# A decoder trunk with a mixture of experts on one core: the gathered rows of experts 2 to 8 turned by VectorE, the router in two products a chunk, constant transposes on TensorE

## The reference, cut to what matters

```python
def moe(xn, w_router, wg, wu, wd):
    t = xn.reshape(-1, D)
    logits = (t @ w_router).astype(jnp.float32)
    top_vals, top_idx = lax.top_k(logits, TOP_K)          # TOP_K = 2 of N_EXPERTS = 8
    gates = jax.nn.softmax(top_vals, axis=-1)
    comb = jnp.einsum('nk,nke->ne', gates, jax.nn.one_hot(top_idx, N_EXPERTS, dtype=jnp.float32))
    for e in range(N_EXPERTS):                            # wg, wu 2048 x 1408, wd 1408 x 2048
        y = y + comb[:, e:e + 1] * swiglu(t, wg[e], wu[e], wd[e])
```

## Time and profile before

| | |
|---|---|
| median of 3 runs | 1921.18 us (1921.08 to 1922.72) |
| the profiled execution: its time | 1918.63 us |
| the profiled execution: its span | 1916.6 us |
| TensorE matmuls, weight loads | busy 1906.1 us (99%), 1587.2 us (83%) |
| VectorE, ScalarE, GpSimd | 1348.1 us (70%), 1160.1 us (61%), 136.6 us (7%) |
| mean granted TensorE clock | 0.999 |
| HBM read, written | 495.33 MB, 13.64 MB: 266 GB/s over the span |

### The profile page before, as it was taken

One profiled execution on the slowest core, in us unless ns is written; L12 is line 12 of the kernel. 1 busy time (PEld: TensorE's weight loads), 2 busy tenths in 40 slices (PEclk: granted clock), 3 DMA queues, 4 the chain that ended last, 5 costly groups with the idle time before them and its releaser, 6 DMA issues.

```text
span 1916.6 us, 25622 instructions
## 1 busy us (share of the span) xinstructions
PE 1906.1 (99%) x8984; PEld 1587.2 (83%) x8984; DVE 1348.1 (70%) x1574; ACT 1160.1 (61%) x1490; POOL 136.6 (7%) x152
## 2 busy tenths in 40 slices
PE   9999999999999999999999999999999999999998
PEld 7888888888888888888888888888888888888887
DVE  8876654545455445444659688898988998988996
ACT  7656543434343344333645567787887878787885
POOL 8300000000000000000200000010100100000101
PEclk9999999999999999999999999999999999999999
DMA  9644555565565555555555468999999999999997
GB/s 357 197 159 161 178 189 191 189 197 187 188 192 192 190 190 190 194 190 188 180 189 167 147 209 319 384 393 388 392 389 393 385 399 380 402 378 401 380 394 259
DMA packets 141571, 510.13 MB, mean 266 GB/s; under 512 B 15937, under 2 KB 15953, under 8 KB 140081
## 3 DMA queue, kind: packets, MB, share of 16 engines
q1 hardware_dynamic: 134288, 486.64, 70.4%
q0 software_dynamic: 7200, 22.39, 4.6%
HBM read 495.33 MB, written 13.64 MB: 266 GB/s over the span
## 4 chain that ended last, share of the span: by engine, by line
PE 98%; DMA 1%; DVE 0%; issue 0%; ACT 0%; SPq 0%; POOLq 0%; DVEq 0%
PE main L617 31%; PE main L619 31%; PE main L618 31%; PE transpose L951 1%; PE transpose L635 1%; PE transpose L816 1%; PE transpose L991 0%; PE transpose L934 0%; DMA raw_pieces<-in_ffn_moe 0%; DMA raw_pieces<-in_w_in 0%; PE transpose L657 0%; DVE w_low L1396 0%; PE transpose L712 0%; PE transpose L713 0%; PE transpose L711 0%
## 5 line engine op out<-in xcount | busy, mean ns | idle before, releaser
L1396 DVE TENSOR_TENSOR w_low<-raw_pieces,w_high 128x1024 fp32r<-128x1024 f32 x919 | 1095.1, 1224 | 420.3 <-ACT w_high L1052 413.8
L1052 ACT ACTIVATE w_high<-raw_pieces 128x1024 fp32r<-128x1024 f32 x919 | 948.2, 1058 | 249.9 <-DMA raw_pieces<-in_ffn_dense 126.2
L617 PE MATMUL main<-w_high,xT_high 128*128 128x512 f32 (+1 forms) x1856 | 719.2, 388 | 0.7 <-DVE w_low L1517 0.3
L619 PE MATMUL main<-w_high,xT_low 128*128 128x512 f32 (+1 forms) x1856 | 710.0, 383 | 0.0
L618 PE MATMUL main<-w_low,xT_high 128*128 128x512 f32 (+1 forms) x1856 | 709.1, 382 | 0.0
L619 PEld LDWEIGHTS main<-w_high,xT_low 128*128 128x128 f32 x1856 | 348.8, 188 | 68.6
L617 PEld LDWEIGHTS main<-w_high,xT_high 128*128 128x128 f32 x1856 | 349.1, 188 | 66.2 <-issue 1.6
L618 PEld LDWEIGHTS main<-w_low,xT_high 128*128 128x128 f32 x1856 | 349.3, 188 | 65.0
L617 PE MATMUL main<-w_high,hT_high 128*128 128x512 f32 x832 | 329.9, 397 | 0.6 <-DVE hT_low L1792 0.6
L619 PE MATMUL main<-w_high,hT_low 128*128 128x512 f32 x832 | 324.6, 390 | 0.0
L618 PE MATMUL main<-w_low,hT_high 128*128 128x512 f32 x832 | 324.1, 390 | 0.0
(11 more groups left out here) (231 smaller groups left out, 816.0 us busy)
## 6 DMA issues: line engine op xcount, KB each, us to landing
raw_pieces<-in_ffn_moe SPq DMA_DIRECT2D x528, 512.0 KB, 6.0
raw_pieces<-in_ffn_dense SPq DMA_DIRECT2D x264, 512.0 KB, 3.5
raw_pieces<-in_w_in SPq DMA_DIRECT2D x96, 512.0 KB, 3.5
raw_pieces<-in_w_out SPq DMA_DIRECT2D x32, 512.0 KB, 3.5
x_resid<-in_x SPq DMA_DIRECT2D x4, 512.0 KB, 14.5
out_x<-x_resid POOLq DMA_DIRECT2D x4, 512.0 KB, 4.5
xn_rows<-token_major POOLq DMA_DIRECT2D x2, 1024.0 KB, 5.5
token_major<-in_x_t SPq DMA_DIRECT2D x1, 1024.0 KB, 9.5
```

Of the source, the lines that this page charges most:

```text
L617: pe.matmul(out_ap, lh[ls], rh[rs], start=first, stop=False)
L619: return pe.matmul(out_ap, ll[ls], rh[rs], start=False, stop=last)
L1052: act.activation(WH[:, piece % RING, :], RAWS[:, piece % RING, :], ACT.Copy).then_inc(high_done, 1)
L1396: dve.tensor_tensor(WL[:, piece % RING, :], RAWS[:, piece % RING, :], WH[:, piece % RING, :], ALU.subtract).then_inc(low_done, 1)
```

## The change

- **Gather.** `xn_rows` has four rows of 2 KB for each token. `XN` is stored with the element inside a chunk first and the chunk second (`p t m k`), so VectorE writes it (L1605 before), ScalarE scales it and TensorE reads it with a step of 16 elements. POOL issues four indirect transfers of 128 quarter-rows instead of one of 128 rows; each takes one quarter of every slot's row, for slots in runs of 32. VectorE turns each quarter in one instruction of 32 x 32 blocks, SBUF to SBUF, into `XTR`, which lies where the low part lies; ScalarE copies two halves of 128 x 1024 as the high part, and VectorE makes the low part in two halves. The 16 transposes on TensorE, and their PSUM banks, are gone from the loop.
- **Row numbers.** `slot_values` makes one more small product pair (4 columns), and VectorE makes a second selection (`SELR`) and one more copy for it at step 8, and a few small tables before the loop.
- **Router.** High and low weights stand side by side in one operand of 16 columns: two products a chunk, the logits' two parts added by two small products each tile. The last block of the output projection runs tile by tile, and its last four chunks are turned per tile through the `main` banks. The last two multiplications with the gain stand later, `keep_busy` writes a `transpose` bank and has two more calls (4 and 7 transposes). ScalarE scales `XN` block by block, and TensorE's first gather waits for each block alone.

```diff
+RUN = 32
+RUNS = P // RUN
+BUSY_LAST, BUSY_COPY, BUSY_RANKS, BUSY_SLOTS = 4, 7, 18, 8
+E_QUARTER = {42: 0, 44: 1, 46: 2, 48: 3}
+E_HALF = {49: 0, 50: 1}
-        XN = TOK[:, 0:TILES * D].rearrange("p (t n) -> p t n", t=TILES)
+        XN = TOK[:, 0:TILES * D].rearrange("p (t m k) -> p t m k", t=TILES, k=KD)
...
-                    pool.indirect_dma_start(XG, None, ROWS[:, :], bass.IndirectOffsetOnAxis(ap=IDX[:, 0:1], axis=0)).then_inc(xg_in, 16)
+                    for i in range(RUNS):
+                        pool.indirect_dma_start(XG[:, i * NB:(i + 1) * NB], None, ROWS[:, :],
+                                                bass.IndirectOffsetOnAxis(ap=IDX[:, i:i + 1], axis=0)).then_inc(xg_in, 16)
...
+                if k < KD - 1:
+                    pe.matmul(both, WRP[:, k, :], high, start=k == 0, stop=False)
+                    return pe.matmul(one, WRH[:, k, :], low, start=False, stop=False)
...
-                    if q == 0:
-                        pe.wait_ge(xg_in, e * 16 + 16)
-                    pe.wait_ge(tp_free, count - 1)
-                    for i in range(4):
-                        c = 4 * q + i
-                        ins = pe.transpose(TP[k % 2][:, i * P:(i + 1) * P], XG[:, c * P:(c + 1) * P], IDN[:, :])
-                    ins.then_inc(tp_ready, 1)
...
+                            if n_pass == 0:
+                                if (i - NEXT_GU) % 4 == 0:
+                                    pe.wait_ge(x_low_done, e * 2 + ((i - NEXT_GU) // 4 + 1))
...
+                        if i in E_HALF and more and n_pass == 0:
+                            half = slice(8 * E_HALF[i], 8 * E_HALF[i] + 8)
+                            act.wait_ge(x_turned, e * RUNS + RUNS)
+                            act.activation(XTH[:, half, 0:SLOTS], XTR[:, half, 0:SLOTS], ACT.Copy).then_inc(x_high_done, 1)
...
+                        if i in E_QUARTER and more and n_pass == 0:
+                            q = E_QUARTER[i]
+                            if q == 0:
+                                dve.wait_ge(xg_in, e * (16 * RUNS) + 16 * RUNS)
+                                dve.wait_ge(used, e * SLICE_PIECES + (s["piece"] + GU_PIECES))
+                            dve.transpose(XTR[:, :, q * RUN:(q + 1) * RUN], XG[:, q * NB:(q + 1) * NB].rearrange(
+                                "p (r k) -> p k r", k=KD)).then_inc(x_turned, 1)
+                        if i - 2 in E_HALF and more and n_pass == 0:
+                            half = slice(8 * E_HALF[i - 2], 8 * E_HALF[i - 2] + 8)
+                            dve.wait_ge(x_high_done, e * 2 + (E_HALF[i - 2] + 1))
+                            dve.tensor_tensor(XTL[:, half, 0:SLOTS], XTR[:, half, 0:SLOTS], XTH[:, half, 0:SLOTS],
+                                              ALU.subtract).then_inc(x_low_done, 1)
```

More of the change, by code:

```diff
@@ L165, in expert_groups @@
     for i in range(SLICE_PIECES):
-        for kind, at in (("t", E_TURN), ("gather", E_GATHER if more else {}), ("st", expert_selt(more, n_pass))):
+        for kind, at in (("t", E_TURN), ("gather", E_GATHER if more and n_pass else {}), ("st", expert_selt(more, n_pass))):
             if i in at:
@@ L232, in trunk @@
         XTH = sb("xT_high", [P, KD, SEQ], F32R)
+        with ExitStack() as scratch:
+            XTR = sb("xT_raw", [P, KD, SEQ], F32, scratch)
         XTL = sb("xT_low", [P, KD, SEQ], F32R)
@@ L885, in _ @@
             for t in range(TILES):
-                ins = pe.transpose(U[1][:, t * N_EXP:(t + 1) * N_EXP], LGT[:, t * P:(t + 1) * P],
-                                   IDN[0:N_EXP, 0:N_EXP])
+                own, rows = U[1][:, t * N_EXP:(t + 1) * N_EXP], LGT[:, t * P:(t + 1) * P]
+                pe.matmul(own, rows, IDN[0:2 * N_EXP, 0:N_EXP], start=True, stop=False)
+                ins = pe.matmul(own, rows, IDN[0:2 * N_EXP, N_EXP:2 * N_EXP], start=False, stop=True)
             ins.then_inc(lg_ready, 1)
@@ L933, in gather, with slot_values @@
                         for t in range(TILES):
-                            ins = pe.matmul(TP[k % 2][:, i * P:(i + 1) * P], XN[:, t, c * P:(c + 1) * P],
+                            ins = pe.matmul(TP[k % 2][:, i * P:(i + 1) * P], XN[:, t, :, c],
                                             SEL[:, t, :], start=t == 0, stop=t == TILES - 1)
                     ins.then_inc(tp_ready, 1)
-                def slot_values():
+                def slot_values(rows):
+                    for t in range(TILES if rows else 0):
+                        pe.matmul(U[0][:, 4:4 + RUNS], SELR[:, t, :], VRUN[:, t, :], start=t == 0, stop=t == TILES - 1)
                     for t in range(TILES):
@@ L1062, in _, with squares @@
             n_square = [0]
-            def squares(d):
-                for t in range(TILES):
+            def squares(d, tiles=range(TILES)):
+                for t in tiles:
                     if n_square[0]:
@@ L1596, in add_out, with times_gain @@
                                              in1=xs, op0=ALU.mult, op1=ALU.add).then_inc(dn_free, 1)
-            def times_gain(d):
+            def times_gain(d, tiles=range(TILES)):
                 cols = slice(d * NB, (d + 1) * NB)
```

184 lines of the change are left out of this document (132 added, 52 removed).

## The result

The changed kernel takes 1923.8 us in the median of 20 runs, the kernel before 1921.05 in 20: a ratio of 1.0016 (95%: 1.0010 to 1.0022), 2.8 us slower, within the 0.2% that the prediction calls no change. Forecast was 1913.5.

A forecast was written before the change was run, and what follows sets the result against it. TensorE, busy 99% of the span, was taken as the bound: -10.4 us of its work, +3 of new waits, 0 before the experts, -7.4 in all, giving a forecast median of 1913.5 us, range 1907.5 to 1928.

The forecast's parts named there:

- Before the experts: Last block, router and first gather: first product of the first expert at about 1157.2 instead of 1157.42; taken as 0.
- What TensorE loses: Experts: TensorE drops groups of four transposes, 0.44 us each; 28 groups in seven experts, 12.3 us gained.
- What it gains in work: Experts: TensorE's added small products for the slot values cost 1.9 us in seven experts, bounds 1.2 and 2.5.
- Does DMA follow?: Experts: transfers need 93.7 us against TensorE's 92.6; after using up a lead, 3 us of new waits, bounds 0 and 5.7.
- the bound of 5.7: Experts: upper limit in us on TensorE's new waits for transfers over seven experts, forecast at 3 us.
- Does VectorE follow?: Experts: with a turn at 0.61 us VectorE has 2.9 us more an expert, 87 of 92.6, so it keeps up.
- the lead at piece 64: Experts: VectorE's low part is ready 5.6 us before TensorE needs it; 3 us taken as what can be eaten once.
- TensorE waits 3.1 us in all for VectorE's low parts: Whole kernel before the change: TensorE's total waiting for these, read as showing that it almost never starves.
- steps of 16 elements are slow: Rival, router and experts: operations on one float32 in 64 bytes slow down, 1927 us at full size; chance 0.24.
- what stores cost: Rival, experts' gather: quarter-rows as dear as stores, 3.5 us more an expert, 1939 us; chance 0.06.
- the marks named in advance: Signs: period 92.6 to 93.1 us, turn near 0.7, first product within 1.5 us of 1157.4, waits up to 6 us.
- SP's 409 us of waiting: Kernel before the change: SP's wait for TensorE to free ring slots, read as a sign that TensorE is the bound.

The follow-up runs named there:

- one_quarter: Changed kernel with VectorE's turn reading neighbouring elements and only the first quarter gathered, one indirect transfer instead of four; 1917.1 us.
- pool_copy_ht: Changed kernel with XN in order, GpSimd's permuted copies, turn in order, and the last activation block's low part ahead of piece 53's; 1908.1 us, ratio 0.9932.
- before_ht: Kernel before the change with only VectorE's low part of the last activation block moved ahead of piece 53's; 1917.1 us, ratio 0.9981.
- strides: Changed kernel with loads, turns and gain multiplication at various element distances, columns permuted; one execution, read for durations only, no total time given.

## Why the prediction was wrong

The step that failed is the last sentence of "Before the experts": "I take 0, bounds -1.5 and +1.5, as long as strides cost nothing". Strides cost: +8.0 us at the first product, measured by its return to 1157.43 with XN in order. A second step failed with it: the turn taken at 0.61 us from an elementwise row, which takes 0.98. Without the 8.0 us the kernel would still have gained 3.4, not 7.4. That 1923.8 lies within 1907.5 to 1928 is owed to the rival alone, for whose sake the range was so wide. Step by step, against the profiled spans (4.6 us apart):

- **What TensorE loses.** A group of four transposes costs 0.48 us, not 0.44: the twelve pieces beside four groups took 18.27 us and take 16.34. 28 groups are 13.5 us.
- **What it gains in work.** The second pair of small products costs 0.44 us (piece 20 takes 2.27 us instead of 1.83), 3.1 us, over my upper bound of 2.5. Both errors cancel: TensorE's period without a listed wait is 92.64 (one_quarter), the 92.6 of the prediction, against 94.10 before, 10.2 us less in seven experts. Both still hold the unlisted 0.2 us at pieces 48 and 49; without it they are 92.45 and 93.92 (pool_copy_ht and before_ht), and the difference is the same.
- **Does DMA follow?** Yes, and the 3 us of new waits for it were wrong. I had a shortfall of transfers of up to 1.1 us an expert. pool_copy_ht runs at 92.48 with all transfers in, so there was none: the 93.7 us of the sum were at least 1.2 too many. Whether the shares of the queues or the 409 GB/s had that wrong, no run separates. The quarter-rows themselves cost nothing that the queue shows: it took 4.5% of the 16 engines' span, 4.6% before.
- **Does VectorE follow?** No. A turn is 0.98 us by distance, not 0.61. What I had only as a wait in the rival is ScalarE's half copy, which stands in its queue before high parts that VectorE wants: the two engines wait for each other. New waits are 0.63 us at the first pieces of each of seven experts, 4.4 us, and 2.3 us nearly all at pieces 42 to 49: 6.7, over the bound of 5.7. The prediction read the lead at piece 64 and called it smaller elsewhere without measuring it; at piece 48 it was 4.6 to 6.2 us in the kernel before. And "TensorE waits 3.1 us in all for VectorE's low parts" left out 0.8 us for the low part of the last activation block, and the 0.2 us an expert that no list names: the bound by order was there already.
- **Before the experts.** Without strides, zero, as forecast. With them +8.0.

Together -10.2 + 4.4 + 2.3 + 8.0 = +4.5, against 4.6. The forecast had -10.4 + 3 + 0.

The rival "steps of 16 elements are slow" was the right one, with a chance of 0.24, and it named the lead's end at about 1.0 us a turn. Its terms were off. ScalarE's scalings, for which it had 4.3 us, cost nothing (709 ns). TensorE's loads, which it had together with the gain at 3 us, cost 6.8: they are not hidden, the gather goes at their pace, and a group of 16 loads takes 3.5 us instead of 1.85. The packets of 2 KB did not cost what stores cost. Of the marks named in advance, the turn "over 1.0: the slow steps", the first product far from 1157.4 and the period above 93.1 spoke. One reading of the rows was too short: SP's 409 us of waiting are of the stretch from 1200 us on, over the whole run it is 1436.6; nothing rests on it.

## What to carry to other kernels

A rearranged view changes no instruction count and no shape, and still changes what each instruction takes: compare the innermost distance in bytes of every operand, engine by engine, and put the permutation where an idle engine or long runs take it. Where two engines are close to each other's pace, the lead that each operation wants is set by what stands ahead of it in its queue: here an urgent small operation behind work for later pieces cost more (4.5 to 6.6 us) than a slow one (1.0 to 3.1). When a visible wait goes and the time stays, look through every expert for where the wait went, and try two remedies at once before a third cause is named. A list of waits that is empty does not say that nothing waits: compare the length of each piece with the shortest.

## What the runs showed of the hardware

- Distance between neighbouring float32 of an operand: 4 or 8 bytes cost the same (weight load 192 and 196 ns, turn of 128 x 512 0.70 us both). At 16 bytes and more it is dearer (12 was not measured): loads 329, 335 and 369 ns at 16, 32 and 48 bytes, and 311 at 64; the turn 1.07, 1.14 and 1.07 us at 16, 32 and 64.
- ScalarE in place on 128 x 512 takes 709 ns at 64 bytes and 710 in order; reading 512 bytes apart, a copy of 128 x 2048 takes 3.73 us, 1.8 ns an element, against 1.04 us for 128 x 1024 in order (L1104 in the changed kernel).
- GpSimd copies 128 x 2048 float32 in runs of 128 bytes in 1.89 us (VectorE was idle for most of it).
- VectorE turns 128 x 512 float32 in blocks of 32 x 32 in 0.70 us, 0.63 by distance (1615.22 to 1615.85 in strides).
- An indirect gather of 1 MB as four transfers of 2 KB rows takes no larger share of the DMA engines than one of 8 KB rows (4.5% against 4.6% of the span for that queue).
